# Two interleaved layer stacks on one core: where the second stack's matrix blocks are placed beside the first's norms

## The reference, cut to what matters

```python
x = first_block(x, ...)                      # even mixer, ffn, odd mixer, ffn
h, hc = x, ctx
for i in range(DEPTH):                       # DEPTH = 2
    m, mc = adaln(c, ada_w[i]), adaln(c_ctx, ada_w[i])
    h  = half_ffn(h,  m,  0, ...)            # the same weights for both streams
    hc = half_ffn(hc, mc, 0, ...)
    u, uc = modulated_norm(h, ...), modulated_norm(hc, ...)
    y, yc = mixer(u, uc, ...)                # x attends to the context's keys and values
    h = gated_residual(h, y, ...);  h = half_ffn(h, m, 6, ...)
    if i < DEPTH - 1:                        # the context ends with its keys and values of layer 1
        hc = gated_residual(hc, yc, ...);  hc = half_ffn(hc, mc, 6, ...)
```

## Time and profile before

| | |
|---|---|
| median of three runs | 2665.64 us |
| profiled execution, its own time | 2669.68 us |
| its span (first to last instruction) | 2667.9 us |
| TensorE busy | 2509.9 us, 94% |
| VectorE busy | 1691.3 us, 63% |
| ScalarE busy | 1250.0 us, 47% |
| mean granted TensorE clock | 0.976 |
| HBM read | 471.48 MB |

### The profile page before, as it was taken

How to read it: one execution, slowest core, us unless ns; L and a number is a source line. 1 busy time by engine, 2 the same in 40 slices (tenths; PEclk the granted TensorE clock), 3 DMA queues, 4 the chain that set the end, 5 groups by cost and what they waited for, 6 DMA issues and landing times.

```text
span 2667.9 us, 48974 instructions
## 1 busy us (share of the span) xinstructions
PE 2509.9 (94%) x20876; PEld 2379.4 (89%) x20876; DVE 1691.3 (63%) x2794; ACT 1250.0 (47%) x1697; POOL 1.2 (0%) x6
## 2 busy tenths in 40 slices
PE   6899998999999999999898999999999999887998
PEld 6799997888998899988887999999999999766997
DVE  5756575656766564566777667576665567656555
ACT  5444453454444444445445555454444345435443
POOL 0000000000000000000000000000000000000000
PEclk9899999999999999999998999999999999898999
DMA  6366656334556655654352344555545555363553
GB/s 223 142 244 242 254 185 220 127 118 147 186 205 235 231 213 205 223 212 167 128 193 80 113 154 164 181 180 175 189 170 179 190 170 183 126 229 139 177 180 119
DMA packets 71591, 480.14 MB, mean 180 GB/s; under 512 B 8784, under 2 KB 9296, under 8 KB 17744
## 3 DMA queue, kind: packets, MB, share of 16 engines
q1 hardware_dynamic: 66240, 468.74, 49.8%
q10 hardware_dynamic: 5136, 8.28, 1.0%
HBM read 471.48 MB, written 1.05 MB: 177 GB/s over the span
## 4 chain that ended last, share of the span: by engine, by line
PE 73%; DVE 14%; ACT 7%; DMA 3%; issue 3%; ACTq 0%; DVEq 0%
PE bank L265 64%; ACT whi L224 4%; DVE wlo L244 3%; DVE wlo L231 2%; PE bank L1144 2%; DMA raw<-w_main 1%; PE bank L1027 1%; DMA raw<-w_down 1%; PE bank L965 1%; DVE ARX L716 1%; DVE HX L662 1%; DVE tmpx L656 1%; PE bank L1015 1%; DMA tmpx<-ARX 0%; PE bank L1710 0%
## 5 line engine op out<-in xcount | busy, mean ns | idle before, releaser
L265 PE MATMUL bank<-HNX_hi,whi 128*128 128x256 f32 x2968 | 860.1, 291 | 43.0 <-DVE wlo L244 17.3
L224 ACT ACTIVATE whi<-raw 128x2048 fp32r<-128x2048 f32 (+1 forms) x378 | 705.3, 1868 | 309.1 <-PE bank L265 155.6
L231 DVE TENSOR_TENSOR wlo<-raw,whi 128x1024 fp32r<-128x1024 f32 (+1 forms) x378 | 453.4, 1199 | 624.9 <-ACT whi L224 623.9
L265 PE MATMUL bank<-HNX_hi,wlo 128*128 128x256 f32 x2968 | 844.7, 286 | 0.0
L265 PE MATMUL bank<-HNX_lo,whi 128*128 128x256 f32 x2968 | 830.5, 285 | 0.0
L265 PEld LDWEIGHTS bank<-HNX_hi,whi 128*128 128x128 f32 x2968 | 577.2, 194 | 68.5 <-issue 37.9
L265 PEld LDWEIGHTS bank<-HNX_hi,wlo 128*128 128x128 f32 x2968 | 577.7, 195 | 0.0
L265 PEld LDWEIGHTS bank<-HNX_lo,whi 128*128 128x128 f32 x2968 | 569.0, 194 | 1.3 <-issue 1.1
L244 DVE TENSOR_TENSOR wlo<-raw,whi 128x1024 fp32r<-128x1024 f32 (+1 forms) x378 | 451.1, 1193 | 0.0
L265 PE MATMUL bank<-HNC_hi,whi 128*128 128x256 f32 x1344 | 390.6, 291 | 9.6 <-DVE tmpc L468 5.7
L265 PE MATMUL bank<-HNC_hi,wlo 128*128 128x256 f32 x1344 | 382.0, 284 | 0.0
(11 more groups left out here) (347 smaller groups left out, 2788.5 us busy)
## 6 DMA issues: line engine op xcount, KB each, us to landing
raw<-w_main SPq DMA_DIRECT2D x270, 1024.0 KB, 4.8
raw<-w_ada SPq DMA_DIRECT2D x72, 1024.0 KB, 4.8
raw<-w_down SPq DMA_DIRECT2D x72, 1024.0 KB, 4.9
raw<-w_down SPq DMA_DIRECT2D x36, 768.0 KB, 4.2
raw<-w_cmp SPq DMA_DIRECT2D x4, 1024.0 KB, 5.5
tmpx<-ARX ACTq DMA_DIRECT2D x18, 128.0 KB, 5.5
tmpx<-ARX ACTq DMA_DIRECT2D x32, 64.0 KB, 4.7
HX<-x_in SPq DMA_DIRECT2D x2, 512.0 KB, 5.9
```

The source lines that it names most:

```text
L224: NS.activation(WHI[q % HIS][:, 0:size], RAW[m % SLOTS][:, 0:size], ACT.Copy).then_inc(sems["w_hi"], 1)
L231: NV.tensor_tensor(WLO[m % SLOTS][:, 0:half], RAW[m % SLOTS][:, 0:half], WHI[q % HIS][:, 0:half].bitcast(fp32), SUB)
L265: return NT.matmul(dst, (WHI[ordinal[n] % HIS], WLO[n % SLOTS])[w][:, k * 2 * P + col:k * 2 * P + col + P], x[xp][:, kx, :], start=start, ...
```

## The change

It has five parts:

1. The condition in `pace` names `kv0` in place of `ffn00`: during x's second feed-forward layer the context is no longer held after its own first feed-forward layer, but only once its layer-0 keys and values have passed.
2. x marks the end of its feed-forward `gu4` (`x_gu4`), and the context waits for that mark, in place of `x_da`, ahead of its last two blocks.
3. In the opening norm the high half of the first weight block is written ahead of the root (`high_only=True`); its low half stays where it was.
4. The `silu` of the conditioning vector moves from behind the root to the end of the opening norm.
5. In lane a's blocks `reach` is 1 in place of 2 during x's second attention (`"ga"` passed) and later.

```diff
-            def splits(n, last=False, most=None, apart=False, reach=3):
+            def splits(n, last=False, most=None, apart=False, reach=3, high_only=False):
@@
                     split_at[0] += 1
+                if high_only:
+                    return
                 while split_at[1] < split_at[0]:
@@ norm
                 first = scale(0) if ahead_of_root else None
+                if opening:
+                    splits(-1, most=1, high_only=True)
                 inv = inverse_root(S, known, hh, rms_h, now(f"{t}_total"))
                 if then is not None:
                     table_of(then)
-                if opening and on(act, in_vec):
-                    NS.activation(CCOL[:, :, 6:8], vec("c").rearrange("p (k s) -> p k s", s=2), ACT.Silu).then_inc(silu_c.sem, 1)
@@ the end of norm
                         los.append(lo)
+                if opening and on(act, in_vec):
+                    NS.activation(CCOL[:, :, 6:8], vec("c").rearrange("p (k s) -> p k s", s=2), ACT.Silu).then_inc(silu_c.sem, 1)
                 if post:
@@ modulation
-                    splits(n, reach=2 if "ga" in passed else 3)
+                    splits(n, reach=1 if "ga" in passed else 3)
@@ pace
-                        if can("c", "D", "d") and not ("ffn00" in passed and urge[0] == 1):
+                        if can("c", "D", "d") and not ("kv0" in passed and urge[0] == 1):
@@ x_sequence
                 yield from ffn(X, 4, post(X, 1, 0), x)
+                passed.add("x_gu4")
@@ c_sequence
                 x = yield from norm(C, True, pre(C, 1, 1), [now("c_evac")], mods)
-                while "x_da" not in passed:
+                while "x_gu4" not in passed:
                     yield ("W",)
```

## The result

| | before | changed |
|---|---|---|
| median of 8 runs each, same chip | 2667.74 us | 2675.11 us |
| profiled execution, its own time | 2669.68 us | 2680.68 us |
| span | 2667.9 us | 2678.9 us |
| TensorE busy | 2509.9 us | 2519.2 us |
| mean granted clock | 0.976 | 0.972 |

The ratio is 1.0026, with a 95% interval of 1.0017 to 1.0035: the change costs 7 us, where a gain of 7 us was forecast. The profiled run of the changed kernel is the longest of its eight, 5.6 us over their median. Both traces have the same 20876 matmuls; the changed kernel's are busy longer because more of them run at the lower clock.

The account below looks back on a forecast made before the run. The prediction took TensorE's stream of blocks, busy 94% of the span, as the bound, so only idle and low-clock time could move. Its terms summed to -7.0 us: 2665.6 - 7.0 = 2658.6 us, range 2647 to 2672.

Parts of the forecast that it names:

- (d): Norm ahead of `gu3`: needs about half its earlier filling, +2 us, between 0 and +6; norm ahead of `gu4` filled as before.
- (a): x's norm ahead of `gu2` loses its five dense context blocks: +12.3 us, bounds +8.8 and +16.3.
- (b): Norm ahead of `da_in` meets the context's own norm and stays open: +2.6 us, between 0 and +8.
- (c): Start of x's first attention: context blocks now fill its places, -15.5 us, bounds -9.6 and -19.6.
- Part 2: Context's last two blocks move from x's `ga_in` into the norm ahead of it: -6.0 us, bounds -12 and 0.
- Parts 3 and 4: Opening norm: first normed tile moves from 16.13 to 15.7 us, -0.4 us, between -1.7 and +1.
- Part 5: x's second attention: ScalarE's split moves one lane-a block later, -2.0 us, between -4 and +1.
- The hold outweighs: Rival: context's small steps delay x's norms, `gu2` 16.3, `da_in` 8, `gu3` 6; sum +6.4, 2672 us; chance 0.17.

Follow-up runs that it names:

- the number let go: Changed kernel, only that many of the context's twelve attention-input blocks run beside x's second feed-forward layer: 2 took 2652.5 us, 6 2662.3, 9 2664.7, 11 2674.5.

## Why the prediction was wrong

**The step that failed is (d)**, "The norm needs about half of what filled it before. +2 us, between 0 and +6. Later the context fills the norm ahead of `gu4` as before". The blocks came as counted, `gu3`'s last gate/up block and three short down blocks. But half of the filling is not half of the loss: the norm lost 13.3 us (+9.8), more than the 11.5 it loses bare. And the context did not recover: the delay between its chunks fell in the norm ahead of `gu4`, which had 144 dense matmuls instead of 240 and cost +8.4 and +2.7 us in the blocks behind. Step (d) was 20.9 us instead of 2; that alone turns -7.0 into +11.9.

The others, in its own order:

- *(a)* right. The norm is 30.7 us long, worked out at 30.1 (+13.0, forecast +12.3).
- *(b)* right in the norm (+2.3, forecast +2.6). It said nothing of x's `da_in`, where six x blocks stand alone before the context's blocks come: +3.1. In the experiments it moved with the number let go: 7.6 us with the kernel before, 8.5 with 2, 18.0, 16.6, 14.6 and 10.7 with 6, 9, 11 and 12.
- *(c)* right and under its value: -19.1, inside its bounds (-19.6), no wait over 0.72 us at the start, clock 1.00.
- *Part 2* had the right length (36.8 us, worked out at 36.2) and the wrong cause. The blocks are worth nothing in the norm; the gain is the context's norm steps leaving it, and that is the hold's doing. Without the hold the part does nothing (1.0002). My own line "the context's small steps follow" had them behind the blocks; it never asked whether the release without the hold would find the context ready.
- *Parts 3 and 4* small as said: the first normed tile is written at 15.49 us (worked out 15.7). *Part 5* -2.5 to -2.8, forecast -2.0: the pair of waits of the earlier trace rows became one of 3.75 us.
- *The rival "The hole outweighs"* had the nearest time, 2672, for another reason: (a) and (b) cost 15.3 together, far from its 24 us, and its 6 us ahead of `gu3` were still too few.

The hold's balance is then: +13.0 and +1.3 in `gu2`, +5.4 around `da_in`, -19.1 in the attention, +20.9 by (d), -2.4 in the transitions of `gu3`, `down3` and `down4`, -7.9 ahead of and in `ga_in`: +11.2 in these stretches, where its own run measured +11.5 to +12.4. Its profiled execution is further off, 14.9 us over that of the kernel before; the second attention (+2.4) and `gu1` (+3.1) are part of the rest.

What stays open: why the norm ahead of `da_in` never filled well, 12 to 16 us at best and 27.6 with two blocks and the context's last attention steps together. The waits name VectorE and ScalarE; no kernel took them apart. Open too is what parts 3 to 5 are really worth: 1.6 to 2.4 us on the kernel before, 7.4 with two blocks let go, of which the traces place 2.1. And open is why five gate/up blocks cost so much more ahead of `gu3` than ahead of `gu4`.

## What to carry to other kernels

When independent work fills the holes of a chain, follow it to every hole behind the change, not only to those that the change names: moving twelve blocks forward emptied two norms some 700 and 1000 us later, and cost more there than at the place they left. Look at the filler's kind and at what its evictions put in front of the chain on the shared engines: in one norm five gate/up blocks left 9.8 us, three down and two gate/up blocks 4.1. And a half-filled hole can cost as much as an empty one, so try an amount between none and all: with the other parts in place, two blocks of twelve gained 15 us where twelve lost 7.

## What the runs showed of the hardware

In the changed kernel's norm ahead of `gu2`, ScalarE switches from the root to the exponential and back; timeline of ScalarE:

```profile
1040.91 1.28 ACT L1944 ACT_TABLE_LOAD   x1
1042.21 0.20 ACT L1944 ACTIVATE SMALL<-SMALL 128x2 f32<-128x2 f32 x1
1042.43 1.28 ACT L551 ACT_TABLE_LOAD   x1
```

Each load takes 1.28 us and starts within 0.03 us of the end of what stands before it. So a switch cost 1.3 us here and not twice that. The Trainium skill ("ScalarE: Activation LUTs", What ACT_TABLE_LOAD costs) adds a drain of 1.38 us to each switch; the trace agrees with its load and has no room for the drain.

Behind a wait of 2.9 us of TensorE part of the next block ran at half clock (in the changed kernel matmuls are 0.21 us apart from 1684 to 1687, 0.12 before and after), so a wait can cost more than its length: the 2.88 and 5.25 us ahead of `gu3` came with some 4 us lost at 1.2 GHz behind them (3.4 and 5.1 us of matmuls at half clock).
